# Group A's probabilities divided by their sums on ScalarE in place of VectorE

## The reference, cut to what matters

```python
s = jnp.einsum('bqngd,bqknd->bqngk', qg, k_sel).astype(jnp.float32) * (HEAD_DIM ** -0.5)
s = jnp.where(valid[:, :, None, None, :], s, -jnp.inf)
p = jax.nn.softmax(s, axis=-1).astype(v_sel.dtype)
o = jnp.einsum('bqngk,bqknd->bqngd', p, v_sel)
```

## Time and profile before

| | |
|---|---|
| time, median of 3 runs | 1733.02 us (1732.82 to 1735.56) |
| span of the profiled execution | 1733.8 us (no other time of it is given) |
| TensorE busy | 92% |
| VectorE busy | 1028.2 us (59%) |
| ScalarE busy | 657.6 us (38%) |
| mean granted TensorE clock | 0.950 |
| attention stage, layer 1 and layer 2 | about 450 to 840 us, 1295 to 1685 us |

### The profile page before, as it was taken

The page is one execution under the profiler, slowest core; times in us unless marked ns, Lnnn a source line. Parts: engine busy times, 40 slices in busy tenths (PEclk is TensorE's granted clock), DMA queues, the critical chain, the costliest instruction groups (busy, mean ns, idle before and its releaser), DMA issues. The chain is left out here.

```text
span 1733.8 us, 19271 instructions
## 1 busy us (share of the span) xinstructions
PE 1600.5 (92%) x6204; PEld 830.5 (48%) x6204; DVE 1028.2 (59%) x2687; ACT 657.6 (38%) x1626; POOL 118.7 (7%) x155
## 2 busy tenths in 40 slices
PE   3999999999889999999879999999997999999992
PEld 1444356566544444443334444665664444444450
DVE  1434526877667777766124443587765767777732
ACT  1223326766533332333112233476563333333322
POOL 0100003300000000000001000131000000000003
PEclk9998999999899999999779999999997999999976
DMA  8111310120411111000051004002004110111005
GB/s 275 44 36 32 128 45 1 52 83 38 171 38 37 37 37 37 18 20 19 18 187 49 23 22 143 25 1 110 38 38 158 37 49 25 37 37 37 19 5 223
DMA packets 80380, 105.22 MB, mean 61 GB/s; under 512 B 18672, under 2 KB 56784, under 8 KB 80208
## 3 DMA queue, kind: packets, MB, share of 16 engines
q1 hardware_dynamic: 80288, 104.04, 17.4%
HBM read 78.48 MB, written 29.97 MB: 63 GB/s over the span
## 5 line engine op out<-in xcount | busy, mean ns | idle before, releaser
L634 PE MATMUL score_ps<-w_slot,hT 128*128 128x512 f32 (+5 forms) x1152 | 436.3, 537 | 9.8 <-DMA w_slot<-in_w_in_dram 5.1
L634 PEld LDWEIGHTS score_ps<-w_slot,hT 128*128 128x128 f32 (+1 forms) x1152 | 209.9, 185 | 222.8 <-issue 214.0
L634 PE MATMUL score_ps<-w_slot,work 128*128 128x512 f32 (+1 forms) x576 | 268.7, 622 | 0.5 <-ACT prob_bm L983 0.5
L970 ACT ACTIVATE hT<-hT,neg_top 128x128 f32<-128x128 f32 (+8 forms) x144 | 118.2, 821 | 379.0 <-DVE neg_top L1219 378.7
L1114 DVE TENSOR_SCALAR_CACHE_REDUCE work<-bias,trial 128x384 f32<-128x384 f32 (+3 forms) x256 | 225.9, 883 | 6.9
L848 ACT ACTIVATE work<-bias,neg_trial 128x768 bf16<-128x768 f32 (+2 forms) x192 | 198.4, 1043 | 64.0 <-DVE neg_trial L1110 64.0
L758 PE MATMUL score_ps<-akT,query_mem 64*128 64x512 f32 (+4 forms) x448 | 193.1, 549 | 13.2 <-ACT prob_bm L983 6.7
L634 PEld LDWEIGHTS score_ps<-w_slot,work 128*128 128x128 f32 (+1 forms) x576 | 106.8, 191 | 149.2 <-issue 148.8
L699 PE MATMUL score_ps<-hT,w_slot 128*128 128x352 f32 x448 | 135.2, 460 | 1.4 <-ACT gate_raw L959 1.4
L1210 DVE CUSTOM_DVE_ANT_0 hT<-score_ps,bias 128x128 f32<-128x128 f32 (+8 forms) x144 | 115.6, 803 | 34.9 <-PE score_ps L758 34.4
L758 PEld LDWEIGHTS score_ps<-akT,query_mem 64*128 64x128 f32 (+1 forms) x448 | 71.8, 184 | 112.4 <-issue 92.3
(11 more groups left out here) (165 smaller groups left out, 1723.3 us busy)
## 6 DMA issues: line engine op xcount, KB each, us to landing
gate_raw<-x_scratch SPq DMA_DIRECT2D x32, 512.0 KB, 3.7
w_slot<-in_w_in_dram SPq DMA_DIRECT2D x8, 2048.0 KB, 9.4
gate_scratch<-gate_raw SPq DMA_DIRECT2D x16, 528.0 KB, 2.7
w_slot<-in_w_out_dram SPq DMA_DIRECT2D x4, 2048.0 KB, 11.0
work<-gate_scratch SPq DMA_DIRECT2D x16, 512.0 KB, 4.6
x_scratch<-gate_raw SPq DMA_DIRECT2D x16, 512.0 KB, 2.6
hT<-x_scratch SPq DMA_DIRECT2D x8, 512.0 KB, 8.1
out_dram<-hT SPq DMA_DIRECT2D x8, 512.0 KB, 4.6
```

The lines of the kernel that those rows point to most:

```text
L634: last = nc.tensor.matmul(out[:, 0:cols], lhs(k), w[:, k, 0:cols], start=(k == 0), stop=(k == KD - 1))
L970: nc.scalar.activation(p, p, ACT.Exp, bias=neg_b[0:r, j:j + 1], scale=SM_SCALE, accum_out=sums[t % 2][0:r, cols]).then_inc(prob_done, 1)
```

## The change

For group A, VectorE's step ends with the reciprocal, which signals a semaphore of its own (`inv_made`). ScalarE, at the place of the `SCALE` step in its own queue, waits for it and copies the probabilities onto themselves with the reciprocal as a per-partition scale, and signals `scaled_a`. B's and M's stay on VectorE and signal `scaled_bm`. TensorE waits on the one or the other. Of both `SCALES_A` and `SCALES_BM` the order in the list is kept.

```diff
--- before.py
+++ after.py
@@ -210,7 +210,8 @@
 
 
 QK_STEPS = [s[1:] for s in STEPS if s[0] == "QK"]
-SCALE_STEPS = [s[1:] for s in STEPS if s[0] == "SCALE"]
+SCALES_A = [s[1:] for s in STEPS if s[0] == "SCALE" and ITEMS[s[1]][1] == "A"]
+SCALES_BM = [s[1:] for s in STEPS if s[0] == "SCALE" and ITEMS[s[1]][1] != "A"]
 
 
 def copied_by_dve(a):
@@ -358,7 +359,9 @@
         neg_top_done = sem("neg_top_done")
         prob_done = sem("prob_done")
         pv_done = sem("pv_done")
-        prob_scaled = sem("prob_scaled")
+        inv_made = sem("inv_made")
+        scaled_a = sem("scaled_a")
+        scaled_bm = sem("scaled_bm")
         mixed_bm = sem("mixed_bm")
         mixed_a = sem("mixed_a")
         x_added = sem("x_added")
@@ -775,7 +778,11 @@
                             i, g = step[1:]
                             t, what, _ = ITEMS[i]
                             if g == 0:
-                                pe.wait_ge(prob_scaled, SCALE_STEPS.index((i, len(score_steps(i)) - 1)) + 1)
+                                last_scale = (i, len(score_steps(i)) - 1)
+                                if what == "A":
+                                    pe.wait_ge(scaled_a, SCALES_A.index(last_scale) + 1)
+                                else:
+                                    pe.wait_ge(scaled_bm, SCALES_BM.index(last_scale) + 1)
                             starts = [1056 * j for j in range(4)] if what == "A" else [256 * n for n in SLOT]
                             p = item_buffers(i)[0]
                             turn(step, 0, [p[0:ROWS[t], starts[h] + P * b:starts[h] + P * b + w]
@@ -984,6 +991,12 @@
                                                            ACT.Exp, bias=neg_b[0:r, slot:slot + 1], scale=SM_SCALE,
                                                            accum_out=sums[t % 2][0:r, col:col + 1])
                             ins.then_inc(free if direct else prob_done, 1)
+                        elif kind == "SCALE" and ITEMS[step[1]][1] == "A":
+                            i, j = step[1:]
+                            t, r, at = ITEMS[i][0], ROWS[ITEMS[i][0]], sum_cols(i, j)
+                            act.wait_ge(inv_made, SCALES_A.index((i, j)) + 1)
+                            p = item_buffers(i)[0][0:r, 1056 * j:1056 * j + NKEYS[t]]
+                            nc.scalar.activation(p, p, ACT.Copy, scale=inv_sum[t % 2][0:r, at]).then_inc(scaled_a, 1)
                         elif kind == "PT" and not copied_by_dve(ATT_GROUP[step[1:]]):
                             a, r = ATT_GROUP[step[1:]], ROWS[ITEMS[step[1]][0]]
                             group = groups_of(ITEMS[step[1]])[step[2]]
@@ -1253,15 +1266,13 @@
                             if what == "B":
                                 link(nc.vector.tensor_tensor(sums[b][0:r, at], sums[b][0:r, at], sink_exp[b][0:r, :],
                                                              ALU.add))
+                            if what == "A":
+                                nc.vector.reciprocal(inv_sum[b][0:r, at], sums[b][0:r, at]).then_inc(inv_made, 1)
+                                continue
                             link(nc.vector.reciprocal(inv_sum[b][0:r, at], sums[b][0:r, at]))
-                            if what == "A":
-                                p = item_buffers(i)[0][0:r, 1056 * j:1056 * j + w]
-                                ins = nc.vector.tensor_scalar(p, p, inv_sum[b][0:r, at], None, ALU.mult)
-                            else:
-                                p = item_buffers(i)[0][0:r, :].rearrange("p (h n) -> p h n", h=4)[:, :, 0:w]
-                                inv = inv_sum[b][0:r, at].rearrange("p (h a) -> p h a", a=1).broadcast_to([r, 4, w])
-                                ins = nc.vector.tensor_tensor(p, p, inv, ALU.mult)
-                            ins.then_inc(prob_scaled, 1)
+                            p = item_buffers(i)[0][0:r, :].rearrange("p (h n) -> p h n", h=4)[:, :, 0:w]
+                            inv = inv_sum[b][0:r, at].rearrange("p (h a) -> p h a", a=1).broadcast_to([r, 4, w])
+                            nc.vector.tensor_tensor(p, p, inv, ALU.mult).then_inc(scaled_bm, 1)
                         elif kind == "PT" and copied_by_dve(ATT_GROUP[step[1:]]):
                             a, r = ATT_GROUP[step[1:]], ROWS[ITEMS[step[1]][0]]
                             group = groups_of(ITEMS[step[1]])[step[2]]
```

## The result

| | before | after |
|---|---|---|
| time, median of 4 runs each, same chip | 1732.92 us (1730.51 to 1735.56) | 1706.15 us (1704.5 to 1708.09) |
| ratio | | 0.9845, 95% interval 0.9815 to 0.9876 |
| span of the profiled execution | 1733.8 us | 1706.3 us |
| mean granted TensorE clock | 0.950 | 0.959 |

The kernel is 26.8 us faster.

What follows compares the result with a forecast made beforehand. TensorE, busy 92% of the span, bounds the kernel; gains come only where it waits or its clock falls. Waits 8.5 us plus clock 6.8 us make 15.3 us off 1733.02: 1717.7 us, range 1709 to 1733.

Steps and rivals of the forecast that it cites:

- Waits of tiles 4 to 6: TensorE's idle times around M's scores shrink by 2.2, 1.2 and 1.05 us a layer as group A's masks come earlier.
- The clock: Attention steps, tiles 4 to 6: four of six falls of TensorE's clock go, 6.8 us; ends 0 and 10.2.
- the brink: TensorE's waits in attention: 1.34 us keeps the clock and 1.39 loses it, so the falls are near their brink.
- Tiles 1 to 3: TensorE's waits: 0.5 us off the 2.64 in tile 1 and 0.36 off the 1.34 in tile 2, a layer.
- The 0.4 for scaled copies ahead of PT copies: ScalarE's queue in tiles 0 to 2: scaled copies ahead of PT copies cost 0.4 us a layer, between 0 and 4.
- The wait at its end: Sample's last item: ScalarE's queue ends at 829.9 in place of 828.4, 1.5 us dearer a layer; wait near 2.2 us.
- the two copies behind exponentials: Sample tile: waits of 0.49 and 0.36 us both go, as masks come 0.76 us earlier; gain 0.85 a layer.
- The price of the scaled copy: On ScalarE: the exponential's price, 0.832 us for 640 keys and 1.18 for 1056; plain copy as lower end.
- A: TensorE in attention: idle times shrink but the clock doesn't come back; 1724.5 us, 1728.8 with half the gain; chance 0.22.
- B: Tiles' waits for M's exponentials: the next wait takes the place, no change, about 1732 us; chance 0.15.
- C: First score step of A items: ScalarE's queue becomes the path, 0.6 us at 36 items, 1746 us; chance 0.14.
- D: ScalarE's scaled copies need another function table, 288 loads of 1.28 us, 2102 us; chance 0.01.

Runs made afterwards that it cites:

- tiles-4-to-6 kernel: Against the changed kernel, ScalarE divides group A only in tiles 4, 5 and 6, VectorE in the other tiles; 1715.05 us.
- the kernel with the multiplications behind the mask: From the kernel before: VectorE still multiplies, but each multiplication is issued behind the next mask addition or M's reduction; 1710.82 us.
- tiles 0, 2, 3 and 7: Against the changed kernel, ScalarE divides group A only in tiles 0, 2, 3 and 7, VectorE in the others; 1729.15 us.
- moving tile 1 alone: Against the changed kernel, ScalarE divides group A only in tile 1, VectorE in the other tiles; 1728.7 us.
- The kernel without the division: The changed kernel with ScalarE's scaled copies left out, so group A's probabilities aren't divided by their sums; 1699.39 us.
- that with tiles 0 to 6: Against the changed kernel, ScalarE divides group A in tiles 0 to 6, VectorE in tile 7 and the sample; 1707.94 us.
- the mixed kernel: Against the changed kernel, ScalarE divides tiles 0 to 6; VectorE multiplies in tile 7 and the sample, behind the next mask; 1702.86 us.
- the waits made by a copy: The changed kernel plus a ScalarE copy ahead of M's exponentials in tiles 4 to 6: 512 elements, 1714.7 us; 1024 elements, 1720.33 us.

## Why the prediction was wrong in size and right in kind

**Waits of tiles 4 to 6: right.** 2.2, 1.2 and 1.05 us were worked out, 4.45 a layer; the idle times shrank by 2.10, 1.38 and 1.04, together 4.52. The tile 4 chain came out step for step: reduction just behind M's product, ScalarE free before M's first exponential. The tiles-4-to-6 kernel shows that nothing else carries this part, and the kernel with the multiplications behind the mask shows why: a multiplication ahead of each mask addition was what made the masks late.

**The clock: the step that failed.** The prediction took four of six falls, 6.8 us, and named 10.2 as the upper end. All six are gone, 10.2 us. And a fall of 3.4 us in tile 1 of each layer (484:492 and 1328:1336) was in no term: it stood behind the wait of 2.64 us at 483.67, whose row had been read for its length only, and no stretch of the clock was read behind it. (A wait of 0.48 us just ahead of it, at 477.2, was left out as well, among those called under 0.3.) The clock's term is 17.0 us in place of 6.8. Shown: with tile 1 divided by VectorE ahead of the masks (before, tiles 4 to 6, tiles 0, 2, 3 and 7) the fall is there in 4 of 6 layers (1.7 us of clock in one, 3.4 in the others); with ScalarE dividing it, or nobody, in none of 18; and moving tile 1 alone gave 4.3 us. Not shown is what in tile 1 decides: its waits are no shorter, and the kernel with the multiplications behind the mask has waits of 0.74 and 0.68 us there and lost the clock in both layers. Nor is there the brink that the prediction saw between 1.34 us, which keeps the clock, and 1.39, which loses it: behind the same wait of 1.34 at tile 2, the tiles-4-to-6 kernel lost 1.7 us in layer 1 (at 511:515).

**Tiles 1 to 3: small errors that cancel.** Tile 1's waits gave nothing (0.5 predicted). Tiles 2 and 3 gave 0.8 in place of 0.36: tile 3 was not in the sum. The 0.4 for scaled copies ahead of PT copies shows in no addition.

**The sample: two terms wrong, which partly cancel.** The wait at its end was foreseen to 0.2 us (2.2 predicted, 2.06 measured, put down to ScalarE). But it was priced at its full length, 1.5 us, with the remark that no clock is lost there; at clock 0.50 it cost half its length, 0.65. And the 0.85 us of the two copies behind exponentials, counted as a gain, came back as 0.47 at tile 7 and 0.79 at the sample, both for a ScalarE copy of PT. The kernel without the division has neither, nor has that with tiles 0 to 6, so it is the scaled copy ahead of the PT copy in ScalarE's queue that delays them. Tile 7 and the sample cost 1.1 us in place of 0.65.

**The sum.** A layer was to give 4.25 + 3.4 = 7.65 us and gave 12.6. The 4.95 between them are 1.7 (the third fall), 2.9 (tile 1's fall less the wait counted there), 0.45 (tiles 2 and 3) and 0.4 (the copies), less 0.45 (the sample).

**The price of the scaled copy: right.** 0.832 us was taken from the exponential for 640 keys, 0.828 measured; 1.18 for 1056, 1.170 measured. The plain copy's lower price (0.15 us less) doesn't hold.

**The rivals.** A (the clock doesn't come back) fell with the windows of after. B (no change) fell with M's first exponential, which starts as early as the reduction lets it. C (ScalarE's queue becomes the path) has its place, tile 7 and the sample, at 1.1 us a layer; the 36 places at 0.6 us it needed don't exist, as taking all scaled copies away changes nothing before tile 7. The Trainium skill's page "ScalarE: Activation LUTs", section "Rules for kernel authors", which says to multiply on VectorE, agrees with these runs in the price of one instruction (0.828 us on ScalarE, 0.553 on VectorE for 640 keys) and not in the kernel's time. What comes nearest to it is the mixed kernel, in which VectorE multiplies where ScalarE's queue is the path, and behind the masks. D (table loads) fell: the trace after has as many table loads as the trace before, and 0.392 us for 128 keys leaves no room for a load of 1.283.

## What to carry to other kernels

Look at what stands between two links of a chain in an engine's in-order queue before you ask how busy the engine is: the gain came from taking 144 operations out from between the mask additions, and moving them a place back on the same engine gave most of it. Before a change to short waits is priced, list the granted clock of every stretch behind every wait that it touches; here the clock was worth twice the waits. A wait inside a stretch that runs at half clock anyway was worth half its length. Where the new engine's queue is itself the end of a chain, leave the operation on the old one, but a place further back.

## What the hardware showed that was not expected

**The clock can fall behind idle times of about 1 to 1.7 us, and not each time.** Each time tiles 4 to 6 of both layers, over all traces: behind waits of 1.39 to 1.71 us in the old order (before, tiles 0, 2, 3 and 7, tile 1) 17 falls in 18; behind the waits made by a copy, 1.39 to 1.51 us, 3 in 6, and 0.95 to 1.08 us, 1 in 6; behind 0.33 to 0.77 us, none in 48. In tiles 1 and 2 falls came behind waits no longer than some of these: in the kernel with the multiplications behind the mask one of 8.5 us right behind a wait of 0.74 us (477.3), and in the tiles 0, 2, 3 and 7 kernel one of 3.4 behind 0.88 (516.5). So the length of the one wait in front doesn't decide. A fall cost 1.7 us in tiles 4 to 6, and mostly 3.4 in tile 1. So a wait on this edge is worth up to twice its length, and its removal pays twice in some executions only.

**Falls of 5 us come and go elsewhere.** One at 154:166 is in five of the thirteen traces, one near 984:1004 in seven, with nothing of the kernels different there. Executions of one kernel lie up to 11 us apart here (1705.44 to 1716.51), and some 9 of these 11 are lost clock (0.961 of 1703.6 us against 0.956 of 1714.7); so two kernels 5 us apart can't be told by four runs each. What sets them off isn't known from these runs.
